# Three attentions of a four-layer block, fused with the projections around them

## The chip, the cores and the metric

The kernel runs on one core of a Trainium2 chip. The metric is the device time of one execution in microseconds, lower is better. In the three runs of the kernel before it took 2087.64, 2087.95 and 2088.01 us, a median of 2087.95 us.

The core has five engines that run their own instruction streams in order and meet only through semaphores: TensorE (PE, matmuls and transposes), VectorE (DVE), ScalarE (ACT), GpSimd (POOL) and SyncE (SP), which here only issues DMAs.

## The reference, cut to what matters

Four layers work on a stream of 512 tokens by 1024 features. What is computed around the change:

```python
# odd layer of the first block (cut)
q, ckv, qi, ki, wi, z = _split(rmsnorm(x) @ w_in, ODD_SPLITS)
k, v = rmsnorm(heads(ckv @ w_uk), g_k), ckv @ w_uv      # 16 heads of 64
score = sum_h(wi * relu(qi @ ki))                       # index, top 128 keys kept
out = softmax(q @ k + bias[t5_bucket] masked to the kept keys) @ v
x = x + (out * silu(z)) @ w_out

# windowed layer with sinks of the second block (cut)
q, k, v = split(rms_norm(h) @ w_qkv + b_qkv)            # 16 heads, 2 key heads, window 128
p = exp(s - m) / (sum(exp(s - m)) + exp(sink - m))
h = h + (p @ v) @ w_o + b_o;   h = h + swiglu(rms_norm(h))

# sparse layer of the second block (cut)
o = g0 * compressed + g1 * selected + g2 * windowed     # three attentions, gated
h = h + o @ w_o;               h = h + swiglu(rms_norm(h))
```

With 512 tokens all blocks are selected and the window covers everything, so the last two branches of the sparse layer are both full causal attentions, over different keys and values.

## The kernel before, in words

**Projections.** Every projection is a `Dense` stage. Activations lie with features on the partitions, 512 tokens in the free direction. Each weight chunk (128 x 1024) is loaded by SP into one of three slots of `raw`, split by ACT into a high part (`split_high`, L1602) and by DVE into the rest (`split_low`, L1611), two chunks ahead of TensorE. For each of 8 slices of the contraction TensorE does three matmuls, rest x high, high x low and high x high (L251 to L253). Results leave the bank by a list of steps on DVE and ACT (`evict`). TensorE may not enter a chunk before `weights_low` has counted it, nor a bank before its old tile's first reader is done.

**Blocks.** `fuse` puts stages one behind the other in one block: each engine runs its part of every stage without meeting the others except by semaphores. At the end of a block all engines meet. The order of blocks before was: one block for the even layer; one for the projections of the odd layer (`odd`, ending in `o_z`); the odd layer's attention; one with `o_out`, `a_q` and `a_kv` (`windowed`); `turn`, a block that transposes the value rows; the windowed attention; one with `a_out`, the first feed-forward, `b_q` and `b_rest` (`sparse`); `compress`; `compressed`; the long attention; one with `b_out`, the second feed-forward and the leaving of results.

**Attention.** `attention` (L1943) goes over 8 head pairs m, in the odd and windowed layer with 4 steps each, one for each 128-query tile in the order t = 3, 1, 2, 0, and in the long one with 8 (two branches). Iteration s of each engine's loop does: TensorE the scores of step s (`score`, L2005, with a masked start L2002 for t = 3 of the odd layer), the transposes of step s - 3 (`turn`, L2016) and the product with the values of step s - 4 (`mix`, L2029); DVE the result of step s - 5 (`finish`, L2077 to L2081), the logits of step s (`logit`, L2062), the reciprocal of step s - 1 (`share`, L2069) and every second copy of transposed probabilities (`keep`, L2089); ACT the exponentials (`exp`, L2139) and the other copies (`keep`, L2148); POOL the division (`divide`, L2111) and, in the odd layer, bias plus mask for t = 1 and 2 (`add_mask`, L2119). SP fetches the bias of a head pair (L1990) in the odd and windowed attention: pairs 0 and 1 when the block begins, pair m when the logits of pair m - 2 are done.

**Behind an attention** `Split` cuts its result `oT` into `o_hi` (ACT, L535) and `o_lo` (DVE, L540), 8 tiles of 128 x 512 in a row; the first matmul of the out-projection waits for the first of them.

**Top keys.** `Cut` finds the 128 best keys by 16 rounds on DVE, laid between the tiles of the projections (`CutBeside`); round 16 comes at tile 6 of `o_z`, and `finish` (L1062), which writes the mask, at tile 7.

Of the kernel before, what the change touches and what calls it, by code (L numbers as in the profile page):

```python
# [28 lines left out]
P = 128  # L29
# [17 lines left out]
            "att_bias0", "att_bias1", "att_scores", "att_logits", "att_probs", "att_dens", "att_ready",  # L47
# [28 lines left out]
class Stage:  # L76
# [5 lines left out]
    def on_act(self, act):  # L82
        pass
# [437 lines left out]


class Split(Stage):


    def __init__(self, k, n, src, hi, lo):
        self.k, self.n, self.src, self.hi, self.lo = k, n, src, hi, lo
        self.high, self.low = k.sig("x_high").take(n), k.sig("x_low").take(n)

    def ready(self, pe, m):  # L530
        pe.wait_ge(self.low.sem, self.low.at(m + 1))

    def on_act(self, act):
        for m in range(self.n):
            self.k.nc.scalar.activation(self.hi(m), self.src(m), ACT.Copy).then_inc(self.high.sem, 1)  # L535

    def on_dve(self, dve):
        for m in range(self.n):
            dve.wait_ge(self.high.sem, self.high.at(m + 1))
            self.k.nc.vector.tensor_tensor(self.lo(m), self.src(m), self.hi(m).bitcast(F32),  # L540
                                           ALU.subtract).then_inc(self.low.sem, 1)
# [497 lines left out]
class Cut(Beside):  # L1039


    def __init__(self, k, index, top, mask, rounds):
        self.k, self.index, self.top, self.mask, self.rounds = k, index, top, mask, rounds
        self.found, self.marked = k.sig("idx_found").take(rounds * 3), k.sig("idx_marked").take(rounds * 3)
        self.n = 0
# [12 lines left out]
    def finish(self, dve):  # L1058
        assert self.n == self.rounds
        for t in range(1, QT):  # L1060
            dve.wait_ge(self.marked.sem, self.marked.at(self.rounds * 3 + t - 3))
            self.k.nc.vector.tensor_scalar(self.mask[:, t, 0:(t + 1) * P], self.index[t][:, :], CUT, -NEG, ALU.not_equal, ALU.mult)  # L1062
# [351 lines left out]

class Kernel:
# [66 lines left out]
    def load(self, pairs):  # L1482
        loads = Loads(self, "small_loads", pairs)
        with self.block() as block:
            @block.sync
            def _(sp):
                loads.on_sp(sp)
                loads.wait(sp)

    def turn(self, tiles, src, dst):  # L1490

        nc, turned, kept = self.nc, self.sig("tile_turned"), self.sig("tile_kept")
        with self.block() as block:
            @block.tensor
            def _(pe):
                for m in range(tiles):

# [1250 lines left out]
```

## Time and profile before

| | |
|---|---|
| median of three runs | 2087.95 us |
| the profiled execution, its time | 2085.21 us |
| its span, first to last instruction | 2083.4 us |
| TensorE busy | 1995.7 us (96%) |
| VectorE busy | 1057.9 us (51%) |
| ScalarE busy | 788.0 us (38%) |
| GpSimd busy | 299.3 us (14%) |
| mean granted TensorE clock | 0.980 |

How to read it: a row of a timeline has the start in us, the duration in us, the engine, the line of the code, the operation with what it writes and reads and its shapes, how many were merged, and in brackets how long the engine had been idle before and who ended that. PEld is the loading of weights into TensorE. A row of a table of windows has the stretch, its length, then busy time and number of instructions of PE, PEld, DVE, ACT and POOL, the mean granted TensorE clock (1.00 is 2.4 GHz, 0.50 is 1.2 GHz), the DMA share and GB/s. A row of the waits says who waited for whom: total us, how many times, the longest.

In the profiled execution the odd layer's attention goes from 680.7 to 765.7 us, the windowed one from 874.1 to 939.4, the long one from 1499.4 to 1650.1.

### The profile page before, as it was taken

To read this page: it belongs to the slowest core of one execution; us is meant where nothing else is said; L and a number is where in the kernel's file an instruction comes from. 1 tells how busy PE (TensorE), PEld (TensorE's weight loads), DVE (VectorE), ACT (ScalarE), POOL (GpSimd) and SP (SyncE) were. 2 spreads that over 40 slices of the span, in tenths; PEclk is the share of its full clock that TensorE was granted. 3 is DMA by queue.
4 is the path that set the end of the run, shared out by engine and by line. 5 is a ranking of instruction groups with operands and counts; after the bars stand their busy time and mean duration, and the time that the engine had idled before them with its cause. 6 is when DMAs were issued, how large, how long until landed. Compare 5 with 4: busy or idle time off the path is not lost. (4 is left out here: it accounts for less than half of the span.)

```text
span 2083.4 us, 25188 instructions
## 1 busy us (share of the span) xinstructions
PE 1995.7 (96%) x9682; PEld 1526.8 (73%) x9682; DVE 1057.9 (51%) x1974; ACT 788.0 (38%) x1391; POOL 299.3 (14%) x392
## 2 busy tenths in 40 slices
PE   7999999999999899899999999998799999999998
PEld 5777778887657567657788888876666678888886
DVE  5467643434579555375544443343366654444322
ACT  3343434433333553364322222223377642222222
POOL 2550000010000641041000000001155310000000
PEclk9999999999999999899999999998699999999999
DMA  7452324343212222213333333355000123333331
GB/s 174 131 162 71 105 78 155 130 149 93 81 51 71 61 62 84 73 27 102 91 94 98 91 94 91 98 143 166 0 2 1 41 83 100 96 97 91 93 91 69
DMA packets 316750, 187.14 MB, mean 90 GB/s; under 512 B 33488, under 2 KB 297168, under 8 KB 316375
## 3 DMA queue, kind: packets, MB, share of 16 engines
q1 hardware_dynamic: 310222, 168.62, 28.8%
q10 hardware_dynamic: 6408, 16.91, 2.1%
q8 instruction: 78, 1.28, 0.3%
q14 instruction: 42, 0.34, 0.0%
HBM read 183.27 MB, written 17.96 MB: 97 GB/s over the span
## 5 line engine op out<-in xcount | busy, mean ns | idle before, releaser
L251 PE MATMUL banks<-xs,wlo 128*128 128x512 f32 x1336 | 539.2, 404 | 5.0 <-PEq L1456 2.8
L253 PE MATMUL banks<-xs,whi 128*128 128x512 f32 x1336 | 529.3, 396 | 0.0
L252 PE MATMUL banks<-xs,whi 128*128 128x512 f32 x1336 | 529.2, 396 | 0.0
L1611 DVE TENSOR_TENSOR wlo<-raw,whi 128x1024 fp32r<-128x1024 f32 (+1 forms) x283 | 359.3, 1270 | 310.9 <-ACT whi L1602 310.7
L1602 ACT ACTIVATE whi<-raw 128x1024 fp32r<-128x1024 f32 (+1 forms) x283 | 293.4, 1038 | 248.7 <-PE banks L253 184.2
L251 PEld LDWEIGHTS banks<-xs,wlo 128*128 128x128 f32 x1336 | 251.7, 188 | 75.4 <-issue 13.1
L252 PEld LDWEIGHTS banks<-xs,whi 128*128 128x128 f32 x1336 | 251.7, 188 | 62.5 <-issue 3.4
L253 PEld LDWEIGHTS banks<-xs,whi 128*128 128x128 f32 x1336 | 251.6, 188 | 60.8
L2139 ACT ACTIVATE prob<-prob,stat 128x384 f32<-128x384 f32 (+5 forms) x256 | 136.5, 534 | 91.2 <-DVE stat L2062 89.0
L413 POOL TENSOR_TENSOR squares<-squares,x_tmp 128x512 f32<-128x512 f32 x35 | 46.9, 1340 | 745.0 <-ACT x_tmp L405 745.0
L251 PE MATMUL banks<-a_hi,wlo 128*128 128x512 f32 x352 | 139.9, 397 | 0.0
L253 PE MATMUL banks<-a_hi,whi 128*128 128x512 f32 x352 | 139.4, 396 | 0.0
L252 PE MATMUL banks<-a_lo,whi 128*128 128x512 f32 x352 | 139.4, 396 | 0.0
L2016 PEld LDWEIGHTS banks<-ident,prob 128*128 128x128 f32 x592 | 64.6, 144 | 54.6 <-issue 51.1
L2016 PE MATMUL banks<-ident,prob 128*128 128x128 f32 x592 | 95.5, 291 | 4.1 <-POOL prob L2111 4.1
L2341 ACT ACTIVATE a_hi<-ff_tmp 128x512 fp32r<-128x512 f32 x44 | 27.8, 632 | 171.5 <-DVE ff_tmp L2340 171.5
L2338 ACT ACTIVATE ff_tmp<-ff_tmp 128x512 f32<-128x512 f32 x44 | 27.8, 632 | 170.2 <-DVE ff_tmp L2337 170.2
L2111 POOL TENSOR_SCALAR prob<-prob,stat,gt_s 128x512 f32<-128x512 f32 (+3 forms) x128 | 76.5, 607 | 96.4 <-DVE stat L2069 96.3
L1637 ACT ACTIVATE xs<-hT,gains 128x512 fp32r<-128x512 f32 x40 | 29.0, 724 | 148.4 <-DVE hT L1631 121.5
L251 PE MATMUL banks<-o_hi,wlo 128*128 128x512 f32 x192 | 77.0, 401 | 6.6 <-DVE o_lo L540 6.6
L2062 DVE CUSTOM_DVE_ANT_0 prob<-banks,bias_all 128x512 f32<-128x512 f32 (+3 forms) x128 | 57.7, 489 | 41.6 <-PE banks L2005 39.0
L253 PEld LDWEIGHTS banks<-a_hi,whi 128*128 128x128 f32 x352 | 66.2, 188 | 16.0
(335 smaller groups left out, 2799.9 us busy)
## 6 DMA issues: line engine op xcount, KB each, us to landing
raw<-in_ffn_w_gu SPq DMA_DIRECT2D x88, 512.0 KB, 3.8
raw<-in_e_w_in SPq DMA_DIRECT2D x56, 512.0 KB, 3.8
raw<-in_ffn_w_down SPq DMA_DIRECT2D x32, 512.0 KB, 4.0
s_skew<-s_bias ACTq DMA_DIRECT2D x6, 2560.0 KB
raw<-in_o_w_in SPq DMA_DIRECT2D x21, 512.0 KB, 4.0
raw<-in_e_w_out SPq DMA_DIRECT2D x16, 512.0 KB, 3.8
raw<-in_b_w_in SPq DMA_DIRECT2D x15, 512.0 KB, 3.8
raw<-in_ffn_w_down SPq DMA_DIRECT2D x16, 384.0 KB, 3.4
```

The lines of the kernel that those rows point to most:

```text
L251: nc.tensor.matmul(out, k.wlo[:, chunk.slot, at, :], self.x_hi(kt), start=first, stop=False)
L252: nc.tensor.matmul(out, k.whi[:, chunk.slot, at, :], self.x_lo(kt), start=False, stop=False)
L253: ins = nc.tensor.matmul(out, k.whi[:, chunk.slot, at, :], self.x_hi(kt), start=False, stop=last)
L413: k.nc.gpsimd.tensor_tensor(k.squares[:, :], k.squares[:, :], k.xtmp[:, n % 2, :], ALU.add).then_inc(self.added.sem, 1)
L1602: self.nc.scalar.activation(self.whi[:, chunk.slot, 0:chunk.blocks, :], self.raw[:, chunk.slot, 0:chunk.blocks, :], ACT.Copy).then_inc(sel ...
L1611: self.nc.vector.tensor_tensor(self.wlo[:, chunk.slot, 0:chunk.blocks, :], self.raw[:, chunk.slot, 0:chunk.blocks, :], hi.bitcast(F32), AL ...
L1637: out += [("act", lambda ps: nc.scalar.activation(self.xs_hi[:, n, :], tile, ACT.Copy, scale=gain)), ("dve", lambda ps: nc.vector.scalar_t ...
L2016: ins = nc.tensor.transpose(T[s % 2][0:r, (2 * b + x) * P:(2 * b + x + 1) * P], probs_of[s % 4][:, x, pad + b * P:pad + b * P + r], self.i ...
L2062: nc.vector.tensor_tensor_reduce(out=pr[:, x, pad:pad + nk], in0=S(s, x)[:, 0:nk], in1=b[:, x, :], scale=1.0, scalar=first, op0=ALU.add, o ...
L2111: nc.gpsimd.tensor_scalar(pr, pr, st[:, s % 4, 2, x:x + 1], g, ALU.mult, ALU.mult).then_inc(ready.sem, 1)
L2139: nc.scalar.activation(pr, pr, ACT.Exp, bias=st[:, s % 4, 0, x:x + 1], scale=-1.0, accum_out=st[:, s % 4, 1, x:x + 1]).then_inc(probs.sem, 1)
L2338: ("act", lambda ps: nc.scalar.activation(tmp[:, 0, :], tmp[:, 0, :], ACT.Silu)),
```

## The change

- `attention` becomes a stage, class `Attention`, that `fuse` can put between projections. One block now holds the odd layer's projections, its attention, `o_out`, `a_kv`, `a_q`, the windowed attention, `a_out`, the first feed-forward and the rest up to `b_rest`; another holds the long attention, `b_out` and what follows. `compress` and `compressed` keep their blocks.
- Biases are fetched by SP as soon as it has issued the last weights of the projection before; they have a place of their own for that, and `Attention` has its own place for the biases plus mask.
- The result of a head pair is split while the attention goes on: ACT does the high part at the end of iteration 4m + 8 (8m + 12 in the long attention), DVE the rest at the end of the iteration after. `Split` is gone. The odd layer writes its result over `zT`.
- The windowed layer projects keys and values (`a_kv`) before the queries (`a_q`); the value rows are transposed beside `a_q` (`TurnValue`), and the block `turn` is gone. The scores of head pair m wait for query tile m.
- The mask is written at tile 6 of `o_z`, behind round 16. In the windowed attention the copy of the sinks stands behind the wait for the scores, not ahead of it.

```diff
+class Attention(Stage):
+    TURN, MIX, FINISH, HIGH, LOW = 3, 4, 5, 5, 6
...
+    def on_sp(self, sp):
+        if self.bias is None:
+            return
+        sp.wait_ge(self.k.sig("bias_spread").sem, 16 * (1 + 2 * 3))
+        for m in range(MT):
+            if m >= 2:
+                sp.wait_ge(self.logits.sem, self.logits.at(2 * self.per_pair * (m - 1)))
...
+        def score(s):
+            m, t, e = steps[s]
+            k0, nk, _ = keys(t)
+            if before is not None and s < 2:
+                pe.wait_ge(evac.sem, before.done(before.tiles - 2 + s, 1))
+            if self.ready_q is not None and s % self.per_pair == 0:
+                self.ready_q(pe, m)
+            pe.wait_ge(self.logits.sem, self.logits.at((s - 1) * 2))
+            masked = self.mask is not None and t > 0 and t not in self.pooled
+            if masked:
+                if s == 0:
+                    self.mask_made(pe)
...
+            dve.wait_ge(self.turned.sem, self.turned.at(s - 3))
+            dve.wait_ge(self.scores.sem, self.scores.at(s + 1))
+            if self.sink is not None:
+                nc.vector.tensor_copy(pr[:, :, 0], self.sink[:, 2 * m:2 * m + 2])
...
+        def split_low(m):
+            dve.wait_ge(self.high.sem, self.high.at(m + 1))
+            nc.vector.tensor_tensor(self.lo(m), self.out(m), self.hi(m).bitcast(F32), ALU.subtract).then_inc(self.low.sem, 1)
+
+        for s in range(self.NS + self.LOW):
+            if 0 <= s - self.FINISH < self.NS:
+                finish(s - self.FINISH)
+            if s < self.NS:
+                logit(s)
+            if 0 <= s - 1 < self.NS:
+                share(s - 1)
+            if 0 <= s - self.TURN < self.NS and (s - self.TURN) % 2 == 1:
+                keep(s - self.TURN)
+            done = s - self.LOW + 1
+            if done > 0 and done % self.per_pair == 0:
+                split_low(done // self.per_pair - 1)
...
+        def split_high(m):
+            act.wait_ge(self.outs.sem, self.outs.at(self.per_pair * (m + 1)))
+            nc.scalar.activation(self.hi(m), self.out(m), ACT.Copy).then_inc(self.high.sem, 1)
+
+        for s in range(self.NS + self.HIGH):
+            if s < self.NS:
+                exp(s)
+            if 0 <= s - self.TURN < self.NS and (s - self.TURN) % 2 == 0:
+                keep(s - self.TURN)
+            done = s - self.HIGH + 1
+            if done > 0 and done % self.per_pair == 0:
+                split_high(done // self.per_pair - 1)
...
+class TurnValue(Beside):
+    def pe(self, pe, n):
+        k = self.k
+        if n == 1:
+            pe.wait_ge(k.sig("tile_steps").sem, self.made)
+            for t in range(QT):
+                ins = k.nc.tensor.transpose(k.ps[4][:, t * P:(t + 1) * P], self.vF[:, t * P:(t + 1) * P], k.ident[:, :])
...
+        project("a_kv", aw, columns(1024, 2))
         project("a_q", aw, columns(0))
-        project("a_kv", aw, columns(1024, 2))
...
-                                    CutBeside(cut, (0, 1, 2, 3, 4, 5, 6), 7)))
+                                    CutBeside(cut, (0, 1, 2, 3, 4, 5, 6), 6)))
...
-                self.fuse(odd_loads, Start(), o_in, gain, o_q, o_uk, o_uv, o_z)
...
+                return [odd_loads, Start(), o_in, gain, o_q, o_uk, o_uv, o_z, attention]
...
-            self.turn(1, lambda m, t: vF[:, t * P:(t + 1) * P], lambda m: vt[:, :, :])
...
+            return [loads, o_out, WindowBias(self, loads, bq, bqs, sink), a_kv, a_q, attention]
...
-                self.fuse(split, a_out, gu, down, b_q, After(self, down), loads, b_rest, Arrived(loads), whole)
+                self.fuse(*stages, a_out, gu, down, b_q, After(self, down), loads, b_rest, Arrived(loads), whole)
...
-            self.fuse(split, b_out, gu, down, Leave(self, rows[0], tok, r, out))
+            self.fuse(attention, b_out, gu, down, Leave(self, rows[0], tok, r, out))
```

## Rows read from the trace of the kernel before

**Rows 1.** Page, part 1: busy time and share of each engine.

```profile
PE 1995.7 (96%) x9682; PEld 1526.8 (73%) x9682; DVE 1057.9 (51%) x1974; ACT 788.0 (38%) x1391; POOL 299.3 (14%) x392
```

**Rows 2.** Waits of TensorE in total; two pieces of the chain behind the long attention.

```profile
PE banks L251 <- DVE o_lo L540: 6.6, 3, 2.2
...
1650.50 0.64 ACT o_hi L535
1651.16 0.70 DVE o_lo L540
```

**Rows 3.** Timeline, end of `o_z` and start of the odd layer's attention, all engines.

```profile
666.37 0.37 SPq L1593 DMA_DIRECT2D raw<-in_o_w_out  x1
...
677.57 1.22 DVE L1611 TENSOR_TENSOR wlo<-raw,whi 128x1024 fp32r<-128x1024 f32 x1
...
678.46 0.40 PE L253 MATMUL banks<-xs,whi 128*128 128x512 f32 x1
678.90 0.69 DVE L2256 TENSOR_TENSOR zT<-banks,row_scale 128x512 f32<-128x512 f32 x1
679.50 0.89 DVE L1062 TENSOR_SCALAR mask<-idx_score 128x256 fp32r<-128x256 f32 x3
679.62 0.63 ACT L2257 ACTIVATE zT<-zT 128x512 f32<-128x512 f32 x1 [4.64 <-DVE zT L2256]
...
680.72 1.28 ACT L2139 ACT_TABLE_LOAD   x1 [0.47 <-PEq L1456]
...
684.28 0.69 DVE L2062 CUSTOM_DVE_ANT_0 prob<-banks,bias 128x512 f32<-128x512 f32 x1 [3.89 <-DMA bias<-s_skew]
...
685.62 0.72 ACT L2139 ACTIVATE prob<-prob,stat 128x512 f32<-128x512 f32 x1 [3.62 <-DVE stat L2062]
```

**Rows 4.** Timeline, end of `a_kv`, `turn`, and start of the windowed attention.

```profile
869.30 0.40 PE L253 MATMUL banks<-xs,whi 128*128 128x512 f32 x1
870.10 0.68 DVE L2304 TENSOR_TENSOR win_tmp<-banks,row_scale 128x512 f32<-128x512 f32 x1
870.82 0.72 ACT L2306 ACTIVATE vF_w<-win_tmp,win_small 128x512 f32<-128x512 f32 x1 [1.89 <-DVE win_tmp L2304]
...
871.90 1.09 PE L1500 MATMUL banks<-ident,vF_w 128*128 128x128 f32 x4 [2.21 <-PEq L1456]
...
876.88 0.17 DVE L2057 COPY prob<-win_small 128x2 f32<-128x2 f32 x1 [3.16 <-DMA bias<-s_skew]
...
877.88 0.51 ACT L2139 ACTIVATE prob<-prob,stat 128x257 f32<-128x257 f32 x1 [2.52 <-DVE stat L2062]
```

**Rows 5.** Timeline inside the odd, windowed and long attention: waits that repeat.

```profile
725.95 0.51 ACT L2139 ACTIVATE prob<-prob,stat 128x256 f32<-128x256 f32 x1 [0.19 <-DVE stat L2062]
...
727.88 0.88 PE L2029 MATMUL banks<-pT,vt 128*64 128x128 f32 x12 [0.32 <-ACT pT L2148]
...
908.48 0.51 ACT L2139 ACTIVATE prob<-prob,stat 128x257 f32<-128x257 f32 x1 [0.82 <-DVE stat L2062]
...
909.35 0.48 DVE L2062 CUSTOM_DVE_ANT_0 prob<-banks,bias,win_small 128x256 f32<-128x256 f32 x1 [0.23 <-PE banks L2005]
...
910.19 0.66 PE L2029 MATMUL banks<-pT,vt_w 128*64 128x128 f32 x8 [0.52 <-ACT pT L2148]
...
1569.37 0.88 PE L2029 MATMUL banks<-pT,vt_s 128*64 128x128 f32 x12 [0.29 <-ACT pT L2148]
```

**Rows 6.** Windows: after the start of two attentions, and of `b_out`.

```profile
684.00:698.00 14.00, 10.37 (x64) 6.33 (x64) 7.26 (x32) 7.93 (x24) 10.76 (x13) 0.76 0.20 67
871.00:887.00 16.00, 11.49 (x58) 7.26 (x60) 7.77 (x39) 7.73 (x24) 3.77 (x9) 0.57 0.18 51
1652.00:1658.00 6.00, 6.00 (x19) 4.77 (x20) 5.20 (x8) 3.71 (x7) 0.00 (x0) 0.72 0.59 168
```

**Rows 7.** Timeline of ScalarE in the even layer, a table load and its first use.

```profile
87.34 1.28 ACT L721 ACT_TABLE_LOAD   x1
88.63 0.63 ACT L721 ACTIVATE gate_rows<-gate_rows 4x512 f32<-4x512 f32 x1
```

More of the change, by code:

```diff
@@ L520, in on_sp @@
         sp.wait_ge(self.stored.sem, 64)
[L523 to L541, printed above, removed]
 class Loads(Stage):
@@ L1480, in _ @@
                     stage.on_pool(pool)
[L1482 to L1496, printed above, removed]
-                    pe.wait_ge(kept.sem, kept.at(m - 1))
-                    for t in range(4):
-                        ins = nc.tensor.transpose(self.banks[:, m % 2, t * P:(t + 1) * P], src(m, t), self.ident[:, :])
-                    ins.then_inc(turned.sem, 1)
-            @block.vector
-            def _(dve):
-                for m in range(tiles):
-                    dve.wait_ge(turned.sem, turned.at(m + 1))
-                    nc.vector.tensor_copy(dst(m), self.ps[m % 2][:, :].rearrange("p (t c) -> p t c", t=4)).then_inc(kept.sem, 1)
-        turned.advance(tiles)
-        kept.advance(tiles)
     def weight_plan(self):
@@ L2175, in odd @@
         with ExitStack() as c2:
+            q_at = self.room_used
             qT = self.sb(c2, "qT", [P, MT, 512])
@@ L2192, in odd @@
                 top = self.sb(c3, "idx_top", [P, QT, 8])
-                rkv = self.sb(c3, "latent_scale", [P, 512])
+                bias = self.place("odd_bias", [P, 2, 2, 512], F32, latent_at)
                 rs = self.xtmp[0:112]
@@ L2295, in windowed @@
             tmp = self.sb(c, "win_tmp", [P, 2, 512])
+            bias = self.sb(c, "win_bias", [P, 2, 2, 256])
+            stat = self.sb(c, "win_stat", [P, 4, 3, 2])
+            o_hi = self.sb(c, "win_hi", [P, MT, 512], F32R)
+            o_lo = self.place("win_lo", [P, MT, 512], F32R, q_at)
             def q_steps(n):
@@ L2348, in feed_forward, with sparse @@
                                  beside=beside)
-    def sparse(self, out):
+    def sparse(self, stages, out):
         nc, d = self.nc, self.d
@@ L2354, in sparse @@
         rb = self.rb[:, :]
-        with ExitStack() as c:
-            split, oh, ol = self.split_out(c)
-            a_out = self.residual("a_out", oh, ol, 4, split.ready, bias=self.win_small[:, 11:19])
+        oh, ol, ready = self.parts
+        a_out = self.residual("a_out", oh, ol, 4, ready, bias=self.win_small[:, 11:19])
         with ExitStack() as c:
@@ L2360, in sparse @@
         with ExitStack() as c2:
+            q_at = self.room_used
             qT = self.sb(c2, "qT_s", [P, MT, 512])
@@ L2683, in build @@
         with ExitStack() as c:
+            k.o_at = k.room_used
             k.oT = k.sb(c, "oT", [P, MT, 512])
             k.win_small = k.sb(c, "win_small", [P, 44])
-            k.odd()
-            k.windowed()
+            stages = k.odd() + k.windowed()
             k.ff_tmp = k.sb(c, "ff_tmp", [P, 2, 512])
-            k.sparse(out)
+            k.sparse(stages, out)
 def _buckets(dist, max_dist):
```

452 lines of the change are left out of this document (224 added, 228 removed).

## The prediction

> **What bounds the kernel.** I read the page's first part, then TensorE's waits, then the timeline around each place where an attention meets a projection, and last one head pair inside each attention. TensorE is busy for 1995.7 of 2083.4 us [rows 1], no other engine for more than 51%, so a microsecond is won only where TensorE stands or runs at its lower clock. The change touches five such seams, called A to E here: A, `o_z` to the odd layer's attention; B, that attention to `o_out`; C, the projections of the windowed layer to its attention; D, that attention to `a_out`; E, the long attention to `b_out`. Two kinds are to be told apart. At B, D and E TensorE stands 2.2 us each, 6.6 us in all, for the first split result [rows 2]. At A and C it stands longer, and what ends the wait last is not the meeting of the engines but a transfer: DVE waits 3.89 and 3.16 us for the bias [rows 3, 4]. Inside the attentions TensorE is nearly dense; once in four steps `mix` waits 0.32, 0.52 or 0.29 us for ACT's copy of transposed probabilities [rows 5].
>
> **Seam A, 3.3 us won.** I follow the chain to the first exponential, which begins at 685.62 [rows 3]; what comes behind it has the same order in both kernels. SP has issued its last weights of `o_z` at 666.37 [rows 3], so the bias is asked for some 14 us before TensorE ends `o_z`. In the kernel before the bias came 3.6 us after the block began (680.72 to 684.28), so even if it stood behind the 512 KB just issued it would be there in time. What is late next: the mask now stands ahead of DVE's split and of the last eviction. DVE: mask at 677.57 for 0.89, split 1.22, eviction 0.69, end at 680.37. ACT: the last silu 0.63, then the table for exp 1.28 [rows 3], so with small gaps the first exponential can begin at 682.3. The scores: TensorE ends `o_z` at 678.7 and has them by about 680.7, the logits are done at 682.0. So ACT decides, 685.62 - 682.3 = 3.3 us. Queued behind the table load is only the first exponential; queued behind DVE's mask is the split of a chunk that TensorE needs only after the attention. POOL's two additions of mask and bias start at about 678.5 and are done before the division wants POOL.
>
> **Seams B, D, E, 2.3 us each.** The barrier and the first split (0.64 and 0.70 us [rows 2]) leave TensorE's path: results of pairs 0 to 6 are split by then, and `o_out` can do 7 of 8 slices of its first tile, 21 matmuls at 0.23 us or 4.9 us, before it needs the last one, which is there some 2 us after the last product. That removes the 2.2 us waits [rows 2] and a tenth in which the last product ended: 6.9 us. The tail of the attention itself (products that wait for single results) stays, since TensorE takes its instructions in order. The out-projection's weights are there, split two chunks ahead as before; the third chunk is now split right behind the attention.
>
> **The clock at E, 1.6 us.** Behind the long attention's gap the granted clock is 0.72 on average over 6 us [rows 6]: with two levels, 2.4 and 1.2 GHz, that is 3.4 us at the lower one, under dense matmuls, half of it lost. What the engine did before it fell: it ended thin products and stood 2.2 us. With the gap gone I expect no fall: 1.6 us won. B and D have the same gap and no fall in the views, so nothing is to be won there.
>
> **Seam C, 4.4 us.** `TurnValue` puts four transposes on TensorE, 1.09 us at the lower clock [rows 4]; bounds 0.55 and 1.1, I take 0.65 as the clock is full there. TensorE then ends the projections at 869.53 + 0.65 = 870.2. DVE evicts the last query tile (0.6 us after TensorE's end as at 870.10, 0.69 long), ACT adds its bias (0.72), then loads the table (1.28): the first exponential at 873.5 against 877.88 [rows 3, 4]. The bias for the logits has come long before, since SP is through with the weights; the scores of pair 0 need only query tile 0. With keys first, ACT has four pieces of eviction in the first tile instead of one. By the timeline it then splits its next chunk 2.4 us later, just when TensorE is about to want it: 0 to 0.3 us lost, I take 0.
>
> Clock behind A and C: half clock for 0.24 x 2 x 14 = 6.7 us and 0.43 x 2 x 16 = 13.8 us [rows 6]. TensorE still has to wait for the first exponential and division at thin work, so I expect the fall to come again, later and shorter; what falls behind the first transposes is about 5 us in both, so 0 in the sum, bounds -1 and +2.5 us at each.
>
> **The splits inside the attentions, 7.9 us lost.** Before, the 24 pairs of splits cost TensorE only the first of each row. Now ACT and DVE do them between steps on which TensorE waits. ACT's 0.64 us stands right behind the exponentials of t = 3. Behind it are queued the exponentials of t = 1 and the copy for `mix` of t = 2, for which TensorE already waits 0.32 us. The slack there is the 0.19 us that ACT was idle [rows 5], so 0.64 - 0.19 = 0.45 us for each split that falls into the running loop: 6 in the odd layer, 2.7 us, and 7 in the long attention, 3.2 us (the last one or two lie in the tail, where ACT and DVE are idle). Bounds: 0, if other slack takes it, and 0.64. In the windowed attention ACT is idle 0.82 us at that point [rows 5] and takes the split for nothing, but DVE has 0.7 us more and idles only 0.23 us a step, so some 0.2 us x 6 = 1.2 us; bounds 0 and 0.7 x 6 = 4.2. The sinks' copy (0.17 us [rows 4]) lay in that same 0.23 us of idle time [rows 5] and now stands behind the scores, 32 times; I take 0.1 us in each of 8 pairs, 0.8 us, bounds 0 and 32 x 0.17 = 5.4. A gain is excluded for both, since nothing is taken from the loop.
>
> **Sum.** Won 3.3 + 6.9 + 1.6 + 4.4 = 16.2, lost 2.7 + 3.2 + 1.2 + 0.8 = 7.9, net 8.3 us. The profiled execution has a span of 2083.4 and a time of 2085.21; it becomes 2075.1 and 2076.9. The median of the runs shown is 2.7 us above that execution, so the median becomes 2087.95 - 8.3 = 2079.7.
>
> **A rule of the skill against it.** A table load takes 1.28 us, and the first use of the table follows it at once: load at 87.34, activation at 88.63 [rows 7]. The Trainium skill, ScalarE: Activation LUTs, section "What ACT_TABLE_LOAD costs", gives about 1283 ns for the load and about 1380 ns of drain besides, 2.66 us for every switch. The trace agrees with the first figure and not with the second. Seams A and C, where the load comes onto the path, would win 1.4 us less each by the page. The sum above goes by the rows.
>
> **Rivals.**
> 1. *The splits are hidden.* For it: ACT is busy 38% and DVE 51% of the span [rows 1], and TensorE runs three to five steps behind the logits. Against it: the repeating waits of `mix` on ACT [rows 5]. Without these costs the gain is 16.2 us, 2071.7, and with a better clock behind A and C up to 5 us more.
> 2. *The splits stop the loop for their whole length* (the slower side). DVE's half waits for ACT's, so the logits of the next step can be held for 0.64 + 0.70 = 1.34 us [rows 2]. 19 of these lie in running loops: 25.5 us lost against 16.2 won, 9.3 slower, 2097.3. The change stops paying from 16.2 / 19 = 0.85 us for each split, and is measurably slower from 20.4 / 19 = 1.07. Against it: DVE waits for TensorE's scores in most steps, so part of the delay is absorbed.
> 3. *The switch of tables costs more than its load.* If ACT emptied itself before it could use the new table, as in no row of this case [rows 7], the first exponentials would come later by about another load's length, 1.3 us at A and C: net 5.7 us, 2082.3. The page named above states such a drain.
> 4. *The fetch is not early.* If the biases still came after the scores (SP held behind weights), 3.3 + 4.4 us would shrink by the waits of 3.89 and 3.16 to almost nothing: net 1.3 us, 2086.7. Against it: SP is free 12 us before the end of `o_z` [rows 3].
>
> **Chances.** The forecast 0.55, rival 1 0.25, rival 2 0.06, rival 3 0.07, rival 4 0.07. A measurement of this kernel can tell about 0.2%, 4.2 us, from no change, so faster means under 2083.8. The forecast's own bounds (splits 0 to 0.64, windowed costs up to 9.6, clock -2 to +5) reach from 2067 to about 2089; nearly all of the forecast's case, all of rival 1 and most of rival 3 are under 2083.8: 0.83. Within 0.2%: rival 4 and the dear end of the forecast: 0.12. Slower: 0.05. The range 2068 to 2086 leaves out the two ends.
>
> **What would show it.** Right: no wait of DVE on the bias at the start of both attentions; the first exponential 3.7 us after the last `o_z` matmul; `o_out`, `a_out` and `b_out` begin within 0.3 us of the last product; full clock behind the long attention; and a repeating wait of `mix` grown from about 0.3 to 0.75 us once in a head pair. Wrong: a head pair of the odd attention still takes the same time (rival 1), or over 1 us more (rival 2); an idle ACT between table load and first exponential with the logits there (rival 3).

## The result, and the profile after

The changed kernel takes 2070.24 us, the median of four runs (2066.21 to 2071.90), against 2087.98 us before: a ratio of 0.9914, 95% interval 0.99 to 0.9929. In a later comparison the same kernel took 2070.94 us (2067.74 to 2071.82, six runs), ratio 0.9919, interval 0.9904 to 0.9933. The forecast was 2079.7 us in a range of 2068 to 2086: the sign and the range held, the gain was under-sized, 8.3 us forecast and 17.7 us measured by medians. The two profiled executions differ by 14.6 us (span 2083.4 and 2068.8, time 2085.21 and 2070.59), and that difference can be followed place by place. The same kernel profiled a second time has a span of 2065.9 us, 17.5 less than before.

The page after, part 1, and the first row of TensorE's waits. They answer to [rows 1] and [rows 2].

```profile
PE 1988.4 (96%) x9682; PEld 1523.5 (74%) x9682; DVE 1059.6 (51%) x1973; ACT 787.2 (38%) x1392; POOL 307.5 (15%) x392
...
PE banks L1511 <- ACT pT L1633: 17.1, 37, 0.8
```

The engines do the same work. The three waits of `o_out`, `a_out` and `b_out` for the first split, 6.6 us in [rows 2], have no row any more. `mix` (L1511) waits longer for ScalarE's copy: 17.1 us in 37 places. In the kernel before this row was 13.9 us in 32 places.

Timeline of the changed kernel at seam A (start, duration, engine, line; in brackets the idle time before and what ended it). It answers to [rows 3].

```profile
678.62 0.89 DVE L1042 TENSOR_SCALAR mask<-idx_score 128x256 fp32r<-128x256 f32 x3
679.42 1.22 DVE L1836 TENSOR_TENSOR wlo<-raw,whi 128x1024 fp32r<-128x1024 f32 x1
679.52 0.39 PE L253 MATMUL banks<-xs,whi 128*128 128x512 f32 x1
680.56 0.69 DVE L2246 TENSOR_TENSOR zT<-banks,row_scale 128x512 f32<-128x512 f32 x1
681.28 0.63 ACT L2247 ACTIVATE zT<-zT 128x512 f32<-128x512 f32 x1 [5.24 <-DVE zT L2246]
681.64 0.69 DVE L1541 CUSTOM_DVE_ANT_0 prob<-banks,odd_bias 128x512 f32<-128x512 f32 x1 [0.39 <-PE banks L1488]
681.93 1.28 ACT L1625 ACT_TABLE_LOAD   x1
...
683.22 0.72 ACT L1625 ACTIVATE prob<-prob,odd_stat 128x512 f32<-128x512 f32 x1
```

DVE no longer waits for the bias. Eviction, silu and table load follow each other, and the first exponential begins 683.22 - 679.52 = 3.70 us after the last `o_z` matmul; before it was 685.62 - 678.46 = 7.16 us [rows 3]. At seam B the out-projection follows the last product at once, while the last pair is still being split:

```profile
763.95 0.44 PE L1511 MATMUL banks<-pT,vt 128*64 128x128 f32 x4 [0.38 <-DVE zT L1559]
...
764.31 0.50 PE L251 MATMUL banks<-odd_hi,wlo 128*128 128x512 f32 x1
...
764.76 0.63 ACT L1637 ACTIVATE odd_hi<-zT 128x512 fp32r<-128x512 f32 x1 [2.22 <-DVE zT L1559]
```

Seam C, which answers to [rows 4]:

```profile
865.85 0.40 PE L253 MATMUL banks<-xs,whi 128*128 128x512 f32 x1
...
866.29 0.69 DVE L2303 SCALAR_TENSOR_TENSOR win_tmp<-banks,row_scale 128x512 f32<-128x512 f32 x1 [1.94 <-PE banks L253]
867.01 0.72 ACT L2304 ACTIVATE qT_w<-win_tmp,win_small 128x512 f32<-128x512 f32 x1 [3.93 <-DVE win_tmp L2303]
...
867.11 0.48 DVE L1541 CUSTOM_DVE_ANT_0 prob<-banks,win_bias,win_small 128x256 f32<-128x256 f32 x1
...
867.75 1.28 ACT L1625 ACT_TABLE_LOAD   x1
...
869.05 0.51 ACT L1625 ACTIVATE prob<-prob,win_stat 128x257 f32<-128x257 f32 x1
```

From the last dense matmul to the first exponential: 3.20 us, before 877.88 - 869.30 = 8.58 us [rows 4]. The table load is the last to end here (the first logit is done at 867.99).

Inside the odd attention the new split (L1637) stands ahead of the exponential of t = 1 and of the copy (L1633) that `mix` waits for; this answers to [rows 5]:

```profile
723.96 0.62 ACT L1637 ACTIVATE odd_hi<-zT 128x512 fp32r<-128x512 f32 x1
...
724.48 0.49 ACT L1625 ACTIVATE prob<-prob,odd_stat 128x256 f32<-128x256 f32 x1
...
725.46 0.79 ACT L1633 ACTIVATE pT<-banks 128x768 f32<-128x768 f32 x1
...
726.39 0.88 PE L1511 MATMUL banks<-pT,vt 128*64 128x128 f32 x12 [0.55 <-ACT pT L1633]
```

Windows behind seam C and at the start of `b_out` (the column before the last two is the granted clock), which answer to [rows 6]:

```profile
866.00:882.00 16.00, 12.95 (x74) 7.45 (x73) 9.66 (x49) 10.20 (x32) 5.38 (x12) 0.72 0.07 18
1639.80:1645.80 6.00, 6.00 (x29) 4.92 (x27) 2.35 (x4) 1.58 (x2) 0.00 (x0) 1.00 0.22 62
```

The table below is worked out from such starts in the two profiled executions. Places follow each other in time. "Last t = 0 score" is the last score of the last head pair, which marks the end of an attention's running loop. Not every difference is of the change: it left the matmuls of the first row alone, and in the row from `a_out` to the long attention's loop 2.0 of the 2.55 us lie in `compress` and `compressed` (from the last matmul of `b_rest` to the first exponential 60.9 and 58.9 us). In the thirteen executions of the changed kernel and its variants the last `o_z` matmul stands anywhere from 676.7 to 682.0 us, and that second stretch takes 57.9 to 60.5 us, each with other pieces at the lower clock. From the first exponential to pair 1 of the windowed attention it is 11.83 us here and 9.42 in the second profile of the same kernel.

| Place | before, us | after, us | won, us | forecast |
|---|---|---|---|---|
| start to last `o_z` matmul (unchanged part) | 678.46 | 679.52 | -1.06 | 0 |
| A: last `o_z` matmul to first exponential | 7.16 | 3.70 | 3.46 | 3.3 |
| first exponential to t = 0 score of pair 1 | 14.31 | 14.56 | -0.25 | 0 |
| odd loop, 6 head pairs | 57.71 | 58.83 | -1.12 | -2.7 |
| B: last t = 0 score to `o_out` | 9.98 | 7.70 | 2.28 | 2.3 |
| `o_out` and the windowed layer's projections | 101.68 | 101.54 | 0.14 | -0.65 |
| C: last dense matmul to first exponential | 8.58 | 3.20 | 5.38 | 5.05 |
| first exponential to t = 0 score of pair 1 | 11.04 | 11.83 | -0.79 | 0 |
| windowed loop, 6 head pairs | 43.73 | 46.26 | -2.53 | -2.0 |
| D: last t = 0 score to `a_out` | 8.63 | 6.50 | 2.13 | 2.3 |
| `a_out` to the long attention's loop | 574.83 | 572.28 | 2.55 | 0 |
| long loop, 14 half pairs | 125.91 | 126.22 | -0.31 | -3.2 |
| E: last t = 0 score to `b_out` | 9.98 | 7.70 | 2.28 | 2.3 |
| `b_out` to the end of the span | 431.4 | 428.96 | 2.44 | 1.6 |
| sum | | | 14.6 | 8.3 |

### The profile page after: what moved, and what is told of

Same layout as the page of the kernel before. It is cut to its first block and busy times, and to the rows that moved or that the text cites. A ratio compares the mean times of both kernels' runs of the same rounds, so it can differ in the third digit from the quotient of the medians.

```text
span 2068.8 us, 25144 instructions
## 1 busy us (share of the span) xinstructions
PE 1988.4 (96%) x9682; PEld 1523.5 (74%) x9682; DVE 1059.6 (51%) x1973; ACT 787.2 (38%) x1392; POOL 307.5 (15%) x392
## 5 line engine op out<-in xcount | busy, mean ns | idle before, releaser
L1597 POOL TENSOR_SCALAR prob<-prob,long_stat,gt_s 128x512 f32<-128x512 f32 (+3 forms) x128 | 79.5, 631 | 91.8 <-DVE long_stat L1547 91.8
L1625 ACT ACTIVATE prob<-prob,long_stat 128x512 f32<-128x512 f32 (+3 forms) x128 | 70.7, 553 | 41.0 <-DVE long_stat L1541 40.1
L252 PEld LDWEIGHTS banks<-a_lo,whi 128*128 128x128 f32 x352 | 66.3, 188 | 15.8
L251 PEld LDWEIGHTS banks<-a_hi,wlo 128*128 128x128 f32 x352 | 66.3, 188 | 15.8
```

What stands on the lines that cost most here:

```text
L251: nc.tensor.matmul(out, k.wlo[:, chunk.slot, at, :], self.x_hi(kt), start=first, stop=False)
L252: nc.tensor.matmul(out, k.whi[:, chunk.slot, at, :], self.x_lo(kt), start=False, stop=False)
L1597: nc.gpsimd.tensor_scalar(pr, pr, self.st[:, s % 4, 2, x:x + 1], g, ALU.mult, ALU.mult).then_inc(self.ready.sem, 1)
L1625: nc.scalar.activation(pr, pr, ACT.Exp, bias=st[:, s % 4, 0, x:x + 1], scale=-1.0, accum_out=st[:, s % 4, 1, x:x + 1]).then_inc(self.probs ...
```

## The experiments

Every kernel is the changed one with the edit shown; medians are beside runs of the kernel before on the same chip. Three of them (DVE's half behind, ScalarE's half twice, places changed) were run once, the others in three or five rounds. A "period" is the distance of two t = 0 scores of neighbouring head pairs; in the long attention a pair is two half pairs, the four steps of each branch. In the steady part of a loop it repeats to 0.01 us, so the periods decide, not the medians: single runs of one kernel lie 2 to 7 us apart.

**Is it the splits that lengthen the loops?** Both halves behind the attention:

```diff
-            if done > 0 and done % self.per_pair == 0:
-                split_high(done // self.per_pair - 1)
+        for m in range(MT):
+            split_high(m)
```

(and the same for `split_low`).

> All eight pairs of splits (ACT's and DVE's) stand behind the attention instead of between its steps; everything is still in one block. My theory (the splits cost the running loop what the two traces differ by: 0.19 us for each head pair in the odd layer, 0.29 in the windowed one with the sinks' copy in it, 0.3 us in all in the long one): the periods of a head pair fall from 9.81 to 9.62 and from 7.58 to between 7.30 and 7.45, and each out-projection begins 1.4 to 1.6 us later behind its attention (0.62 + 0.70 for the first split, with the signals between), so seams B, D and E take 9.1 to 9.3 us from the last t=0 score instead of 6.5 to 7.7. Net about 1.5 to 3 us slower than the changed kernel, near 2072. Rival 1 (the splits in the loop were free, the longer periods come from something else of the change): the periods stay 9.81 and 7.58, net 4.5 us slower. Rival 2 (the seams' gain came from the barriers alone, not from where the splits stand): seams stay within 0.3 us of the changed kernel's, net 2 to 3 us faster.

Measured: 2069.33 us, ratio 0.9923 (0.9903 to 0.9943). Odd period 9.58 instead of 9.81: the splits cost 0.22 us for each pair there. The half pairs of the long attention that took 9.11 now take 8.89, but every fourth takes 9.08 to 9.10; the loop is 1.0 us shorter. But the windowed period did not move:

```profile
898.23 0.49 PE L1488 MATMUL banks<-kT_w,qT_w 64*128 64x128 f32 x4
...
905.80 0.49 PE L1488 MATMUL banks<-kT_w,qT_w 64*128 64x128 f32 x4
```

905.80 - 898.23 = 7.57 us with no split in the loop. My theory was right for the odd and the long attention and wrong for the windowed one, where the splits are free. The out-projections began 1.15 us later at each seam (8.85, 7.65 and 8.86 us from the last t = 0 score), less than the 1.4 to 1.6 expected. So rival 2 does not hold, and rival 1 holds for the windowed layer alone. The placing of the splits gives about what it takes: 3 x 1.15 us at the seams against 1.3 + 1.0 us in the loops. The loss of 1.5 to 3 us that I expected does not show in the median.

**Which engine's half, and why?** Three edits. DVE's half alone behind the attention:

> Only DVE's halves of the splits stand behind the attention; ACT's stay in the loop where the change put them. It asks which engine's half costs the 0.22 us for each head pair of the odd layer. My theory (ACT's half, ahead of its copy for mix of t = 2): the odd period stays 9.80 to 9.81, every other quad of the long attention stays 9.11, the windowed period stays 7.58. Rival (DVE's half delays the next logits): the odd period falls to 9.58 and the long attention's quads to 8.89.

Measured: odd period 9.81, windowed 7.58, long 9.11 at every pair's end, as in the changed kernel; 2070.91 us. DVE's half costs the loops nothing. On the contrary: with it gone from the long loop, every fourth half pair takes 9.08 to 9.10 us, as with both halves behind, where the changed kernel has 8.89, and the loop is 0.6 us longer (126.81 against 126.22). ScalarE's half made twice:

```diff
+            nc.scalar.activation(self.hi(m), self.out(m), ACT.Copy).then_inc(self.twice.sem, 1)
+            act.wait_ge(self.twice.sem, self.twice.at(m + 1))
             nc.scalar.activation(self.hi(m), self.out(m), ACT.Copy).then_inc(self.high.sem, 1)
```

> ACT makes its half of each split twice, one behind the other, in the same place of the loop. My theory (in the odd layer the slack is used up, so a second one costs its whole length, in the windowed layer ACT has idle time to give): the odd period goes from 9.81 to between 10.3 and 10.5, every other quad of the long attention from 9.11 to between 9.6 and 9.8, the windowed period stays within 0.1 us of 7.58. Rival (the cost of the first was a fixed one, of a signal or of the order, and not its length): the periods stay within 0.1 us.

Measured, two neighbouring t = 0 scores of the odd attention:

```profile
729.34 0.49 PE L1489 MATMUL banks<-kT,qT 64*128 64x128 f32 x4
...
739.81 0.49 PE L1489 MATMUL banks<-kT,qT 64*128 64x128 f32 x4
```

A period of 10.47 us, 0.66 more, and 9.77 instead of 9.11 in the long attention: once the slack is gone the full length is paid. It is the full 0.6 us and not less because the edit makes the second split wait for the first: it begins at 736.55, when the first, from 735.90, has ended. The windowed period rose to 7.93, by 0.35, where I had expected under 0.1: its slack takes one split and about half of a second. The third edit puts both halves one step later, `HIGH, LOW = 6, 7` for `5, 6`, so that ScalarE splits behind the copy for `mix`:

> ACT's split comes one step later (behind its copy of transposed probabilities of t = 2, instead of ahead of it), DVE's one step later too. My theory (in the odd layer the split stands ahead of the copy that mix of t = 2 waits for, and that is all it costs): the period of a head pair in the odd layer goes from 9.81 back to 9.62 to 9.68, and mix's longest wait on ACT's copy from 0.55 back to about 0.32 us; the windowed layer stays at 7.5 to 7.6. About 1 us faster than the changed kernel, too little for the median to show, so the periods in the trace decide. Rival (the split costs engine time wherever it stands, since ACT's next exponentials are what the loop waits for): the period stays at 9.78 or above.

```profile
725.04 0.62 ACT L1637 ACTIVATE odd_hi<-zT 128x512 fp32r<-128x512 f32 x1
...
725.28 0.88 PE L1511 MATMUL banks<-pT,vt 128*64 128x128 f32 x12 [0.32 <-ACT pT L1633]
...
726.09 0.49 PE L1488 MATMUL banks<-kT,qT 64*128 64x128 f32 x4
```

`mix` waits 0.32 us again, as in [rows 5], and the odd period is 9.58, all 0.22 us back. The long attention went to 8.89 throughout (14 half pairs in 124.66 us instead of 126.22). In the windowed layer the period rose to 7.92, which I had not expected: the same split is free one step earlier and costs 0.34 us here. Which engine's half does it was not tried. Seams became 0.2 to 0.66 us longer, since the last pair is split later too. Median 2069.93 us, ratio 0.9913 (0.9894 to 0.9932).

**What lengthens the windowed loop?** The sinks' copy back ahead of the wait for the scores:

```diff
-            dve.wait_ge(self.scores.sem, self.scores.at(s + 1))
             if self.sink is not None:
                 nc.vector.tensor_copy(pr[:, :, 0], self.sink[:, 2 * m:2 * m + 2])
+            dve.wait_ge(self.scores.sem, self.scores.at(s + 1))
```

> The copy of the sinks into the logits' tile stands ahead of DVE's wait for the scores again, as in the kernel before; nothing else differs. My theory, after the run with the splits behind (period 7.58 with no split in the loop): the whole longer period of the windowed layer is this copy, so it goes from 7.58 to 7.29 us, about 2 us less over the layer. Rival (it is the fused block's other placing of tiles, or the biases' tile): the period stays 7.5 or more.

```profile
897.44 0.49 PE L1488 MATMUL banks<-kT_w,qT_w 64*128 64x128 f32 x4
...
899.15 0.16 DVE L1537 COPY prob<-win_small 128x2 f32<-128x2 f32 x1
...
899.58 0.48 DVE L1541 CUSTOM_DVE_ANT_0 prob<-banks,win_bias,win_small 128x256 f32<-128x256 f32 x1 [0.27 <-PE banks L1488]
...
904.73 0.49 PE L1488 MATMUL banks<-kT_w,qT_w 64*128 64x128 f32 x4
```

The copy runs while DVE would idle, and the period is 904.73 - 897.44 = 7.29 us, that of the kernel before. The whole 0.29 us was this copy of two columns. On the chain from score to logit it puts the logit back by 0.07 to 0.11 us; from score to score two of the four steps of a pair are 0.14 us longer with it (2.06 for 1.92, 2.33 for 2.18) and the other two are not. 2067.59 us, ratio 0.9908 (0.9892 to 0.9924).

**A and C: the transfer, the order, or the barrier?** SP asks for the biases only when the tile ahead has been evicted:

```diff
+        sp.wait_ge(self.k.sig("tile_steps").sem, self.before.done())
         for m in range(MT):
```

> SP asks for the attention's biases only when the last tile ahead of it has been evicted, as at a block's start; all else as in the changed kernel. My theory (at A and C the bias transfer was the last wait to end, 3.6 us from asking to landing): the first exponential comes 7.2 us after the last o_z matmul instead of 3.70, and 5.5 to 6.0 us after the last dense matmul of the windowed layer's projections instead of 3.20; DVE waits for the bias in both; together 5.8 to 6.4 us slower than the changed kernel, about 2076.5. Rival (the barrier was what cost at A and C and the transfer was hidden behind the exponential table's load and the scores): the first exponential moves by under 1 us at each, 2071 to 2072.

```profile
685.33 0.69 DVE L1542 CUSTOM_DVE_ANT_0 prob<-banks,odd_bias 128x512 f32<-128x512 f32 x1 [4.32 <-DMA odd_bias<-s_skew]
...
874.10 0.17 DVE L1539 COPY prob<-win_small 128x2 f32<-128x2 f32 x1 [3.76 <-DMA win_bias<-s_skew]
```

The first exponentials begin 7.40 and 5.88 us after the last dense matmul instead of 3.70 and 3.20 (686.68 and 875.10 against 679.28 and 869.22), so 3.70 and 2.68 us are lost, 6.4 in all, with no barrier anywhere near. At A that is everything the change won. 2075.38 us, ratio 0.9946 (0.9931 to 0.996). The order of the windowed layer's projections undone (`a_q` ahead of `a_kv`, the four transposes between `a_kv` and the attention):

> In the windowed layer the queries are projected before keys and values again, and the four transposes of the values stand between the projections and the attention, in one block with both; biases still ahead. My theory (the order is worth only what the last tile's chain costs: eviction by DVE and ACT, then the transposes, then scores): the first exponential comes 4.4 to 4.8 us after the last dense matmul instead of 3.20, and the query row wins back the 0.35 us of transposes, so 0.9 to 1.3 us lost at C; the median about 2071.3, not told from the changed kernel. Rival (keys and values first carries most of C's 5.4 us): the first exponential comes 6 us or more after the last dense matmul.

```profile
864.28 0.72 ACT L2310 ACTIVATE vF_w<-win_tmp,win_small 128x512 f32<-128x512 f32 x1 [1.89 <-DVE win_tmp L2308]
865.05 0.66 PE L1661 MATMUL banks<-ident,vF_w 128*128 128x128 f32 x4 [1.91 <-ACT vF_w L2310]
...
866.35 1.28 ACT L1625 ACT_TABLE_LOAD   x1
...
867.64 0.51 ACT L1625 ACTIVATE prob<-prob,win_stat 128x257 f32<-128x257 f32 x1
```

The last dense matmul began at 862.75, so the first exponential comes after 4.89 us, just over the 4.4 to 4.8 expected and 1.69 later than with keys and values first, and the rows of projections took 0.43 us less: the order is worth 1.7 us at the seam, 1.3 net, and the early transfer 2.7 us. What is left of C's 5.4 us, 5.38 - 2.68 - 1.69 = 1.0 us, I put down to the barriers, which I did not try alone; nor is it shown that the three add up. 2068.32 us, ratio 0.9913 (0.9897 to 0.993), not told from the changed kernel, as expected.

**B, D and E: what is the fusion worth, and whose is the clock?** The blocks are cut behind the three attentions:

> The block boundaries (a barrier of all engines) come back behind the three attentions, at B, D and E alone; the splits stay in the loop, A and C stay fused. My theory (the fusion there is worth that the last product, its finish, the last split and the barrier are no longer ahead of the out-projection): each out-projection begins 1.7 to 2.5 us later behind its attention than in the changed kernel, 5 to 7 us in all, near 2076; and the granted clock behind the long attention falls again as in the kernel before (0.7 instead of 1.00 over the first 6 us of b_out), 1.5 us more. Rival (the clock at E has nothing to do with the gap): the seams cost the same, the clock stays 1.00 behind E.

The windows are the first 6 us of `o_out`, `a_out` and `b_out`:

```profile
766.60:772.60 6.00, 6.00 (x19) 4.77 (x20) 1.23 (x1) 0.92 (x1) 0.00 (x0) 0.72 0.52 83
938.00:944.00 6.00, 6.00 (x19) 4.77 (x20) 1.23 (x1) 0.93 (x1) 0.00 (x0) 0.72 0.89 241
1647.10:1653.10 6.00, 5.96 (x19) 4.79 (x20) 1.23 (x1) 0.98 (x1) 0.00 (x0) 0.72 0.90 239
```

Each seam takes 2.34 us longer (10.04, 8.84, 10.04), and behind all three gaps the granted clock falls to 0.72 on average, 19 matmuls in 6 us where the changed kernel does 28 or 29. That costs 1.5 us each: the stretch from `o_out` to the last projection rises from 101.54 to 103.09 us. 2080.29 us, ratio 0.9967 (0.9952 to 0.9982), 10 us slower than the changed kernel and 4 more than I had expected, for I had the fall at E alone. That it came at all three is what this one execution shows; see the clock below.

**The pace of the out-projections.** High and low parts change places in memory in the windowed and the long attention:

> High and low parts of the results change places in memory in the windowed and the long attention; the same instructions in the same order. If the pace of an out-projection (24 products of 128x512: 5.62 us everywhere in the kernel before, 5.55, 5.57 and 5.50 in the changed one) comes from where its moving operands lie, the paces of a_out and b_out change by 0.03 us or more each; if it comes from the fusion or from what the other engines do at the time, they stay 5.57 and 5.50.

The start of the second and of the eighth tile of `b_out` in the changed kernel:

```profile
1645.46 0.39 PE L251 MATMUL banks<-long_hi,wlo 128*128 128x512 f32 x1
...
1678.42 0.39 PE L251 MATMUL banks<-long_hi,wlo 128*128 128x512 f32 x1
```

32.96 / 6 = 5.49 us for a tile of 24 matmuls. With the places changed the same two rows stand at 1639.99 and 1673.38: 5.57 us, where every other variant has 5.49. `a_out` kept its 5.57 us, though its three kinds of matmul took other shares of it (0.235, 0.231 and 0.231 us from start to start became 0.230, 0.233 and 0.233). So with other places the pace of `b_out` is another, by 1.3%, but half of what I expected did not come. And the places are not the whole rule: in three of the variants (DVE's half behind, both halves a step later, and the combined one with the earlier eviction) `a_out` runs at 5.55 us a tile, in all others at 5.57, and none of these edits moves an operand. What sets the pace is open.

**A better version.** The splits of all but the last pair one step later in the odd and the long attention, the sinks' copy ahead of the wait, and one small exponential in the middle of `a_q`, so that the table for exp is there before seam C:

```diff
+        if n == 4:
+            k.nc.scalar.activation(self.stat[:, 0, 1, 0:1], self.vF[:, 0:1], ACT.Exp)
```

It ran twice, first with the eviction ahead of the split of weights in `o_z` as well, then without it, beside the changed kernel.

> The changed kernel with: splits of all but the last head pair one step later in the odd and the long attention (not in the windowed one), the sinks' copy ahead of the scores' wait, one small exponential by ACT in the middle of the windowed layer's query projections so that the table is loaded before seam C, and in o_z the eviction ahead of the split of weights. Terms, all from runs: odd 0.22 x 6 = 1.3, long 1.6, windowed 0.29 x 7 = 2.0, seam C up to 1.0 (the table load of 1.28 leaves the path, logits at 867.99 decide instead), seam A 0.3: 6 us faster than the changed kernel, 2064. Rival: the part that is won at C is given back by a longer low clock, 2065; if a table had to be loaded anew by the copies behind the small exponential, C gains nothing.

> The changed kernel as it is, beside the combined versions on one chip. All theories: a ratio to the kernel before of 0.990 to 0.993, periods 9.81, 7.58 and 9.11 / 8.89 by turns; its median against the next run's gives the gain of the combination.

> The combined version without the earlier eviction in o_z, which won nothing at seam A (the table load began 2.40 us behind the last product with it and 2.41 without). Periods 9.58, 7.29 and 8.89, first exponential of the windowed layer about 2.0 us behind the last dense product. By the terms of its parts 1.3 + 1.6 + 2.0 + 1.2 = 6 us faster than the changed kernel of this same call, a ratio to the kernel before of about 0.988; rival (the parts are given back by the clock): under 3 us.

Measured: 2061.84 us, ratio 0.9878 (0.986 to 0.9897); then 2062.83 us, 0.9878 (0.9858 to 0.9898), beside 2070.94 us for the changed kernel. By medians that is 8.1 us less, where 6 were expected; single runs of either spread over 2 to 4 us. The two profiled executions differ by 4.5 us (spans 2061.4 and 2065.9), so the parts do not explain why the medians differ by more. Periods are 9.58, 7.29 and 8.89 us. The earlier eviction won nothing, and where 0.3 us were expected of it, it lost 1.1. The table load began 2.40 us behind the last matmul with it and without it, but the first exponential came 4.82 us behind it (686.80 and 681.99) instead of 3.70. DVE's split of the weights then stood ahead of the first logit, and took 1.92 us beside POOL's additions (1.22 ahead of them in the other version), so the exponential waited 1.13 us for DVE. ScalarE around seam C:

```profile
850.35 1.28 ACT L1671 ACT_TABLE_LOAD   x1
...
866.41 0.72 ACT L2307 ACTIVATE qT_w<-win_tmp,win_small 128x512 f32<-128x512 f32 x1 [3.93 <-DVE win_tmp L2306]
867.29 0.51 ACT L1626 ACTIVATE prob<-prob,win_stat 128x257 f32<-128x257 f32 x1 [0.15 <-DVE win_stat L1542]
```

The exponential now comes 2.04 us after the last dense matmul (865.25) instead of 3.20, and the copies and biased copies between the two need no table of their own.

## Why the prediction was right or wrong

**Seams A, B, D, E: right.** 3.46 against 3.3; 2.28, 2.13 and 2.28 against 2.3 each. (One reading at A was off without effect: from 666.37 to the end of `o_z` at 678.7 there are 12 us, not 14.) The step that named the transfer as A's last wait was confirmed by the late fetch, which took back all of it (3.70 us). The cut blocks took back the others.

**Seam C: right in kind, 0.6 us too small.** 5.38 us gross against 5.05 and, for the transposes, 0.43 us against 0.65 (that tile of `a_q` takes 6.03 us instead of 5.60). The step took DVE's eviction as late as in the kernel before, 0.80 us behind the start of the last matmul (870.10 and 869.30 [rows 4]); it came 0.44 behind.

**"The splits inside the attentions, 7.9 us": the step that failed.** The table has 4.0 in the three loops, of which 0.8 is a stretch of lower clock in the windowed one (its second period is 8.38 us, and 7.58 when the kernel was profiled again), so the splits and the copy cost 3.2. For ScalarE's split I took its duration, 0.64 us, less the idle time shown, 0.19. In the trace the split moves the next instruction by 0.52 us, start to start (723.96 to 724.48), because neighbours on ScalarE overlap, and for the same reason the slack is larger than the idle time shown, about 0.3. What is left is the 0.22 us that the periods show. So: odd 6 x 0.22 = 1.3 for 2.7, long 7 x 0.22 = 1.5 for 3.2. In the long attention 1.2 of this was hidden, because the kernel before lost 0.36 us in every fourth half pair (9.25 instead of 8.89), with DVE idle 0.4 us for nothing that the profile shows; the changed kernel loses 0.19 in the first of the loop and nothing in the others. Taking DVE's half alone out of the loop brings a loss of 0.19 back in every fourth, so it is that half that hides it; by what means is open. As a sign of this step I had named a wait of `mix` of 0.75 us; it is 0.55, the same step too dear by the same 0.2.

**Windowed: the sum near, its parts wrong, and so by luck.** I had 1.2 us for DVE's splits and 0.8 for the sinks' copy. The splits cost nothing and the copy 6 x 0.29 = 1.7 us, 2.0 forecast. I had divided one idle time of DVE between two users by their lengths. What counts is on which side of the wait they stand: the split comes behind the logits, the copy between score and logit.

**The clock.** At E the forecast 1.6 us is in the measured 2.44. The experiments widen this step: with results split in the loop and no barrier, none of 30 seams B, D and E in ten executions shows a clock under 1.00 in its first 6 us; with a wait of TensorE ahead, of 1.1 to 2.3 us (the kernel before, the cut blocks, both halves behind, DVE's half behind), 6 of 12 do, each for some 1.5 us. B and D of the kernel before happened to show none, and from that I concluded that nothing was to be won there. It was one execution. Medians are taken over such executions, and this is the likeliest reason why they differ by more (17.7 and 15.9 us) than the first two profiles (14.6). That part is argued, but the second profile of the changed kernel bears it out: 17.5.

Behind C I took 0 with bounds of -1 and +2.5. The first profile lost 0.79 + 0.8 us there (clock 0.72 over 16 us). The same kernel, profiled again, has 1.00 in that window, and the time from the last dense matmul to pair 1 is 12.62 instead of 15.03 us; its windowed loop is 0.8 shorter too. Against the kernel before that is 1.6 us won behind C, inside the bounds, where the first profile's loss of 1.6 us is outside them. Over the kernels here the clock in those 16 us is between 0.68 and 1.00. So this term belongs to the execution and not to the change, and could only be given a width.

**Not foreseen: the pace of the out-projections**, 5.62 us for each tile before and 5.55, 5.57 and 5.49 after, 1.9 us in all. The change moved the operands, and I read the diff of `place` for overlaps in time and not for this; that the places are the cause is shown in part only.

**The shortfall as a whole.** 8.3 us were forecast and 17.5 measured between the profile before and the second one after. Of the 9.2 us between them 4.7 are the splits and the copy (7.9 forecast, 3.2 paid), 1.9 the pace and 0.6 seam C. The remaining 2 us are the net of stretches of lower clock: +1.6 behind C, +2.0 from `compress` to pair 1 of the long attention, -1.1 up to the last `o_z` matmul, -0.3 behind A. So half of the shortfall is the failed step, and the range held although the dear splits, the pace and seam C all erred to the same side. Its dear end was also added up wrong: with splits of 0.64, windowed costs of 9.6 and the clock at -2 the sum gives 2091.7, not about 2089.

**The rivals.** Rival 1 (splits hidden) came nearest, 2071.7 against 2070.2, and is half true: the windowed splits are hidden, those of the other two attentions are not. That its number fits is luck, since 3.2 us that it denies were paid and more than that came from elsewhere. Rival 2's price for each split would have been 1.34 us; 0.22 was measured, and 0.66 for a second one that waits for the first. Rival 3 is refuted: at A, C and in [rows 7] the exponential starts 1.29 or 1.30 us after its table load began. The drain of 1380 ns in the Trainium skill ("ScalarE: Activation LUTs", section "What ACT_TABLE_LOAD costs") is in none of the three places. Rival 4 was built as the late fetch: 2075.4 where it had 2086.7, for a late bias takes back the seams A and C and not the other gains.

## What to carry to other kernels

Fetch what the first step behind a barrier needs ahead of the barrier, then look at what ends the wait last: here the transfer was worth 2.7 and 3.7 us at a seam, the barrier 2.3 and the table load 1.2. An instruction put into a tight loop is priced by start-to-start distances and by which wait it stands ahead of, not by its duration and the engine's share of busy time: in the windowed loop 0.16 us of copy between score and logit cost 0.29 us a pair, and 0.6 + 0.7 us of splits behind them nothing. And a stretch of low clock seen, or not seen, in one execution is a chance and not a term.

## What the runs showed of the hardware

- A DVE `tensor_tensor` with two inputs in memory took 1.00 us beside POOL's division and 0.69 us alone (765.42, `odd_lo`). POOL's two divisions of that step took 1.79 us together, and 1.36 us where no split ran. Taken singly:

```profile
743.98 0.69 POOL L1597 TENSOR_SCALAR prob<-prob,odd_stat 128x512 f32<-128x512 f32 x1 [0.99 <-DVE odd_stat L1547]
...
744.21 1.00 DVE L1572 TENSOR_TENSOR odd_lo<-zT,odd_hi 128x512 fp32r<-128x512 f32 x1 [0.32 <-ACT odd_hi L1637]
...
744.65 1.12 POOL L1597 TENSOR_SCALAR prob<-prob,odd_stat 128x512 f32<-128x512 f32 x1
```

  POOL's first, which began first, took its 0.69 us as if alone; DVE's, begun 0.23 us into it, took 0.31 more, and POOL's second, begun 0.56 us before DVE's end, took 0.43 more. The Trainium skill, "SBUF — State Buffer", section "Who interferes with whom", says that such a pair contends and calls it an exclusive lock. The order of the three agrees with that: each is held up by the one ahead of it, and the first by none.
- A matmul of 512 columns started 0.226 to 0.235 us after its neighbour on average, at the full clock, in the three out-projections of the kernels here. The averages repeat from tile to tile and mostly from kernel to kernel; part of the difference came with other places of the moving operands, part came without.
- The clock fell behind waits of TensorE as short as 1.1 us (2 of 6) and behind 2.2 to 2.3 us (4 of 6), within the first 6 us of dense matmuls, and behind none of the 30 seams without a wait.
- Behind a small exponential no table was loaded for six copies and biased copies and the exponentials after them, though the first exponential came 15.6 us later (851.65 to 867.29).
